# Two 192-slot experts in a mixture-of-experts decoder: high and low token halves in one 128-column stationary

## The reference

```
logits = (x2d @ router_w).astype(jnp.float32) + router_b.astype(jnp.float32)
top_val, top_idx = lax.top_k(logits, TOP_K)        # TOP_K = 2 of 8
gates = jax.nn.softmax(top_val, axis=-1)
...
    return swiglu(xb, w_gate[e], w_up[e], w_down[e])   # silu(h @ gate) * (h @ up) @ down
...
out = jnp.zeros((n + 1, d), ys.dtype).at[slot_tok].add(ys)
```

## Time and profile before

| what | value |
|---|---|
| median of 3 runs | 1949.5 us (1949.02 to 1953.09) |
| profiled execution | 1946.6 us, its span 1945.0 us |
| busy share of the span | PE 91%, PEld 81%, DVE 53%, ACT 40%, POOL 24% |
| mean granted TensorE clock over the span | 0.948 of full speed |
| first expert matmul, last store of an expert's rows | 1342.0 us, 1915.1 us |

### The profile page before, as it was taken

The page is one execution under the profiler, slowest core; times in us unless marked ns, Lnnn a source line. Parts: engine busy times, 40 slices in busy tenths (PEclk is TensorE's granted clock), DMA queues, the critical chain, the costliest instruction groups (busy, mean ns, idle before and its releaser), DMA issues.

```text
span 1945.0 us, 29426 instructions
## 1 busy us (share of the span) xinstructions
PE 1761.2 (91%) x10972; PEld 1582.8 (81%) x10972; DVE 1027.2 (53%) x1427; ACT 784.4 (40%) x1116; POOL 470.0 (24%) x1201
## 2 busy tenths in 40 slices
PE   5798998998999999998899889964999999999993
PEld 4688897998999999998777777743888888888882
DVE  5556544635333233325565546444755945855785
ACT  4244424223232232223244234224644744754773
POOL 5867881002000000006678840010000000000001
PEclk8798999998999999998879899996999999999997
DMA  3521222247223222224312222318956965975994
GB/s 120 99 69 52 69 66 74 86 133 271 87 86 96 88 88 87 95 86 136 67 48 79 66 77 76 121 33 325 355 176 213 374 232 187 368 248 180 336 370 174
DMA packets 124091, 291.35 MB, mean 150 GB/s; under 512 B 31024, under 2 KB 31152, under 8 KB 123840
## 3 DMA queue, kind: packets, MB, share of 16 engines
q1 hardware_dynamic: 90576, 241.38, 36.1%
q0 software_dynamic: 9376, 33.07, 4.7%
q10 hardware_dynamic: 24016, 15.25, 3.7%
HBM read 261.14 MB, written 28.51 MB: 149 GB/s over the span
## 4 chain that ended last, share of the span: by engine, by line
PE 76%; DVE 8%; ACT 5%; issue 5%; DMA 3%; ACTq 2%; POOL 0%; SPq 0%; POOLq 0%; DVEq 0%
PE acc L1511 39%; PE acc L1748 9%; PE acc L1749 8%; PE acc L1750 8%; PE side L1511 2%; PE side L1595 2%; PE acc L1541 1%; ACTq L814 1%; DMA uu<-u_d 1%; ACT wh L670 1%; DMA xg_d<-hn_tok,idx 1%; PE side L1519 1%; DVE rs L1037 1%; PE side L1793 1%; PE side L1618 1%
## 5 line engine op out<-in xcount | busy, mean ns | idle before, releaser
L1019 DVE TENSOR_TENSOR mwl<-mraw,mwh 128x1024 fp32r<-128x1024 f32 x288 | 338.1, 1221 | 117.4 <-ACT mwh L934 116.1
L1511 PE MATMUL acc<-xh,wh 128*128 128x264 f32 (+1 forms) x1600 | 381.8, 309 | 5.6 <-DVE wl L1019 2.5
L1511 PE MATMUL acc<-xl,wh 128*128 128x264 f32 (+1 forms) x1600 | 373.4, 303 | 0.0
L1511 PE MATMUL acc<-xh,wl 128*128 128x264 f32 (+1 forms) x1600 | 371.8, 302 | 0.0
L1019 DVE TENSOR_TENSOR wl<-raw,wh 128x512 fp32r<-128x512 f32 x328 | 217.9, 706 | 267.2 <-ACT wh L670 262.5
L934 ACT ACTIVATE mwh<-mraw 128x1024 fp32r<-128x1024 f32 x288 | 288.6, 1054 | 100.6 <-PE acc L1750 86.4
L1511 PEld LDWEIGHTS acc<-xh,wh 128*128 128x128 f32 x1600 | 260.6, 191 | 25.9 <-issue 11.8
L1511 PEld LDWEIGHTS acc<-xl,wh 128*128 128x128 f32 x1600 | 259.5, 191 | 10.4 <-issue 1.2
L1511 PEld LDWEIGHTS acc<-xh,wl 128*128 128x128 f32 x1600 | 258.6, 191 | 10.2
L670 ACT ACTIVATE wh<-raw 128x512 fp32r<-128x512 f32 x328 | 187.4, 621 | 186.7 <-PE acc L1511 143.2
L1748 PE MATMUL acc<-mwh,xth 128*128 128x512 f32 x528 | 208.4, 395 | 7.3 <-ACT ytok L980 4.8
(11 more groups left out here) (345 smaller groups left out, 2789.2 us busy)
## 6 DMA issues: line engine op xcount, KB each, us to landing
mraw<-in_W SPq DMA_DIRECT2D x288, 512.0 KB, 5.2
raw<-in_W SPq DMA_DIRECT2D x328, 256.0 KB, 2.7
xg_d<-zero POOLq DMA_DIRECT2D x15, 512.0 KB, 9.8
xt<-xg_d POOLq DMA_DIRECT2D x11, 512.0 KB, 6.9
yg_d<-ytok POOLq DMA_DIRECT2D x11, 512.0 KB, 3.7
hs<-in_xT SPq DMA_DIRECT2D x8, 264.0 KB, 4.7
u_d<-uperm ACTq DMA_DIRECT2D x8, 264.0 KB, 2.0
uu<-u_d ACTq DMA_DIRECT2D x16, 132.0 KB, 6.5
```

What stands on the lines that cost most here:

```text
L1019: return v.tensor_tensor(out, a, b, op)
L1511: ins = mm(out, w, x[:, t0:t1], start=first and i == 0, stop=last and i == 2)
```

## The change

Ranks 1 and 2 get 192 slots instead of 256: a full tile and a half tile of 64 tokens (HALF). rows_in(b, t) tells a tile's rows. In the half tile the low parts lie in columns 64 to 127 of xth and hth, beside the high parts in columns 0 to 63, so that one 128-column stationary holds both. The sums of rows 64 to 127 (low part times high weights) belong to the tokens of rows 0 to 63, and are added to them later, on the way to silu, to hb and to ytok. The routing arithmetic follows the new capacities, and up to five extra tiles (was four) can follow.

```diff
-CAPS = tuple(n * TOK for n in NT)
+HALF = TOK // 2
+CAPS = (2 * TOK, TOK + HALF, TOK + HALF) + (TOK,) * (EXPERTS - 3)
-EXTRA = 4
-SLOTS = (TILES + EXTRA) * TOK
+EXTRA = 5
+FIRST_EXTRA = sum(CAPS)
+SLOTS = FIRST_EXTRA + EXTRA * TOK
...
+        part = place("part", [HALF, 2, HCOLS], at=[UU()[0], UU()[1]])
+        def rows_in(b, t):
+            return min(TOK, CAPS[ORDER[b]] - t * TOK) if isinstance(b, int) and b < EXPERTS else TOK
...
@@ gpsimd @@
+                    pool.dma_start(xt[0:n, t, :], rows(xg_d, at + t * TOK, n)).then_inc(xt_landed[t], 16)
...
@@ scalar @@
+                            if r == HALF:
+                                a.activation(part[:, 0, :], acc[HALF:TOK, 0, 1, :], ACT.Copy).then_inc(upper_ready, 1)
+                                act.wait_ge(part_ready, halves_before(b) * CH + c + 1)
+                            a.activation(sg[0:r, x, :], part[:, 0, :] if r == HALF else acc[:, 0, t, :], ACT.Silu)\
+                                .then_inc(silu_ready, 1)
+                    if j in MUL_AT and rows_in(b, nt - 1) == HALF:
+                        arrived(j)
+                        a.activation(part[:, 1, :], acc[HALF:TOK, 1, 1, :], ACT.Copy).then_inc(upper_ready, 1)
...
+                    if rows_in(b, t) == HALF:
+                        arrived(U_MOE - 1)
+                        a.activation(ytok[0:HALF, x, :].rearrange("p (b c) -> p b c", b=2), moe_sums(nt, t)[HALF:TOK],
+                                     ACT.Copy).then_inc(upper_ready, 1)
+                        continue
...
@@ vector, routing @@
-            v.tensor_scalar(baseE[k], rankE[k], float(WIDE), float(TOK), ALU.min, ALU.mult)
-            link(v.tensor_scalar(capE[k], rankE[k], float(WIDE), float(TOK), ALU.is_lt, ALU.mult))
+            v.tensor_scalar(baseE[k], rankE[k], 3.0, float(HALF), ALU.min, ALU.mult)
+            v.tensor_scalar(xtmp[k], rankE[k], 1.0, float(HALF), ALU.min, ALU.mult)
+            v.tensor_scalar(capE[k], rankE[k], 3.0, float(HALF), ALU.is_lt, ALU.mult)
+            link(v.tensor_scalar(extra[k], rankE[k], 1.0, float(HALF), ALU.is_lt, ALU.mult))
+            tt(baseE[k], baseE[k], xtmp[k], ALU.add)
+            link(tt(capE[k], capE[k], extra[k], ALU.add))
...
+            v.tensor_scalar(incl[k], xtmp[k], float(2 * TOK), 0.0, ALU.is_gt, ALU.add)
             link(tt(extra[k], extra[k], ebase[k], ALU.add))
+            link(tt(extra[k], extra[k], incl[k], ALU.add))
...
@@ vector, expert blocks @@
+                low = xtl[:, t, :, :] if r == TOK else xth[:, t, :, HALF:TOK]
...
+                    if j in SILU_AT and rows_in(b, nt - 1) == HALF:
+                        dve.wait_ge(upper_ready, halves_before(b) * (2 * CH + 1) + SILU_AT.index(j) * 2 + 1)
+                        tt(part[:, 0, :], part[:, 0, :], acc[0:HALF, 0, 1, :], ALU.add).then_inc(part_ready, 1)
...
+                            if r == HALF:
+                                dve.wait_ge(upper_ready, halves_before(b) * (2 * CH + 1) + c * 2 + 2)
+                                link(tt(part[:, 1, :], part[:, 1, :], acc[0:HALF, 1, 1, :], ALU.add))
+                            tt(hb[0:r, x, :], sg[0:r, x, :], part[:, 1, :] if r == HALF else acc[:, 1, t, :], ALU.mult)\
+                                .then_inc(hidden_ready, 1)
...
+                if rows_in(b, nt - 1) == HALF:
+                    x = (tb + 1) % 2
+                    dve.wait_ge(ytok_ready, tb + 1)
+                    dve.wait_ge(upper_ready, (halves_before(b) + 1) * (2 * CH + 1))
+                    y2 = ytok[0:HALF, x, :].rearrange("p (b c) -> p b c", b=2)
+                    tt(y2, y2, moe_sums(nt, 1)[0:HALF], ALU.add).then_inc(ytok_ready, 1)
...
@@ tensor @@
+                    ins = nc.tensor.transpose(side[:, m // 4, m % 4 * P:m % 4 * P + r], xt[0:r, t, m * P:(m + 1) * P],
+                                              ident[0:r, 0:r])
...
-                def product(out, w, cols, hi, lo, first, last):
-
+                def product(out, w, cols, hi, lo, r, first, last):
+
+                    if r == HALF:
+                        if first:
+                            mm(out, hi, mwh[w][:, cols], start=True, stop=False)
+                        ins = mm(out[0:HALF], hi[:, 0:HALF], mwl[w][:, cols], start=False, stop=False)
+                        return ins if first else mm(out, hi, mwh[w][:, cols], start=False, stop=last)
                     mm(out, hi, mwh[w][:, cols], start=first, stop=False)
                     mm(out, lo, mwh[w][:, cols], start=False, stop=False)
                     return mm(out, hi, mwl[w][:, cols], start=False, stop=last)
```

More of the change, by code:

```diff
@@ L513, in _ @@
                         pool.dma_start(xg_d[z:z + n, :], zero[0:n, :]).then_inc(zeroed, 16)
-                    for z in range(TILES * TOK, SLOTS, P):
+                    for z in range(FIRST_EXTRA, SLOTS, P):
                         n = min(P, SLOTS - z)
@@ L608, in _, with rows @@
             pool.wait_ge(scattered, 2 * TB * 16)
-            def rows(d, at):
-                return d[at:at + TOK, :] if isinstance(at, int) else d[bass.ds(at, TOK), :]
+            def rows(d, at, n=TOK):
+                return d[at:at + n, :] if isinstance(at, int) else d[bass.ds(at, n), :]
             def load(b, tb, nt, at):
@@ L617, in load @@
                 for t in range(nt):
-                    pool.dma_start(xt[:, t, :], rows(xg_d, at + t * TOK)).then_inc(xt_landed[t], 16)
+                    n = rows_in(b, t)
+                    pool.dma_start(xt[0:n, t, :], rows(xg_d, at + t * TOK, n)).then_inc(xt_landed[t], 16)
             load(0, 0, NT[ORDER[0]], BASE[ORDER[0]])
@@ L625, in _ @@
                     pool.wait_ge(ytok_ready, tb + t + 1)
-                    pool.dma_start(rows(yg_d, BASE[ORDER[b]] + t * TOK), ytok[:, (tb + t) % 2, :])\
+                    n = rows_in(b, t)
+                    pool.dma_start(rows(yg_d, BASE[ORDER[b]] + t * TOK, n), ytok[0:n, (tb + t) % 2, :])\
                         .then_inc(y_stored[(tb + t) % 2], 16)
@@ L631, in _ @@
                 with pool.Fori(0, n_extra) as i:
-                    at = i * TOK + TILES * TOK
+                    at = i * TOK + FIRST_EXTRA
                     pool.wait_ge(xt_turned, i + TILES)
@@ L934, in wide_hi_of, with gather_hi @@
                 a.activation(mwh[w][:, :], mraw[j % RAWS][:, :], ACT.Copy).then_inc(wide_hi[w], 1)
-            def gather_hi(n, t):
+            def gather_hi(n, t, r=TOK):
                 act.wait_ge(xt_turned, n + 1)
-                a.activation(xth[:, t, :, :].rearrange("p (b k) s -> p b (k s)", b=2), side[:, 0:2, :], ACT.Copy)\
+                a.activation(xth[:, t, :, 0:r].rearrange("p (b k) s -> p b k s", b=2),
+                             side[:, 0:2, :].rearrange("p b (k s) -> p b k s", k=4)[:, :, :, 0:r], ACT.Copy)\
                     .then_inc(xth_ready, 1)
@@ L963, in moe_block @@
                             act.wait_ge(hidden_turned, n + 1)
-                            a.activation(hth[:, t, 4 * c:4 * c + 4, :].rearrange("p k s -> p (k s)"), side[:, 2 + x, :],
+                            r = rows_in(b, t)
+                            a.activation(hth[:, t, 4 * c:4 * c + 4, 0:r],
+                                         side[:, 2 + x, :].rearrange("p (k s) -> p k s", k=4)[:, :, 0:r],
                                          ACT.Copy).then_inc(hth_ready, 1)
@@ L1381, in _ @@
             link(v.tensor_scalar(ebase[k], xtmp[k], float(TOK), 0.0, ALU.is_gt, ALU.add))
+            v.tensor_scalar(incl[k], xtmp[k], float(2 * TOK), 0.0, ALU.is_gt, ALU.add)
             link(tt(extra[k], extra[k], ebase[k], ALU.add))
+            link(tt(extra[k], extra[k], incl[k], ALU.add))
             link(v.tensor_tensor_scan(incl[k], oneE[k], extra[k], 0.0, ALU.mult, ALU.add))
             link(tt(ebase[k], incl[k], extra[k], ALU.subtract))
-            link(v.tensor_scalar(xtmp[k], ebase[k], float(TOK), float(TILES * TOK), ALU.mult, ALU.add))
+            link(v.tensor_scalar(xtmp[k], ebase[k], float(TOK), float(FIRST_EXTRA), ALU.mult, ALU.add))
             link(tt(xtmp[k], xtmp[k], capE[k], ALU.subtract))
@@ L1419, in wide_lo_of, with gather_lo @@
                 tt(mwl[w][:, :], mraw[j % RAWS][:, :], mwh[w][:, :].bitcast(F32), ALU.subtract).then_inc(wide_lo[w], 1)
-            def gather_lo(n, t):
+            def gather_lo(n, t, r=TOK):
                 dve.wait_ge(xth_ready, n + 1)
-                as2 = lambda x: x[:, t, :, :].rearrange("p (b k) s -> p b (k s)", b=2)
-                tt(as2(xtl), side[:, 0:2, :], as2(xth).bitcast(F32), ALU.subtract).then_inc(xtl_ready, 1)
+                as2 = lambda x: x.rearrange("p (b k) s -> p b k s", b=2)
+                low = xtl[:, t, :, :] if r == TOK else xth[:, t, :, HALF:TOK]
+                tt(as2(low), side[:, 0:2, :].rearrange("p b (k s) -> p b k s", k=4)[:, :, :, 0:r],
+                   as2(xth[:, t, :, 0:r].bitcast(F32)), ALU.subtract).then_inc(xtl_ready, 1)
             def moe_block(b, tb, nt, nxt, slack=1):
```

(10 more changed lines are left out.)

27 lines of the change are left out of this document (15 added, 12 removed).

## The result

The kernel after takes 1928.4 us (median of 4 runs, 1922.7 to 1930.5) against 1951.3 for the kernel before in the same comparison: ratio 0.9875, 95% interval 0.9858 to 0.9892. Timed again with five runs, it was 1922.9 us and 0.9851 (0.9835 to 0.9867). It is faster by 1.2 to 1.5%, 23 to 28 us; 14 us slower was forecast.

A forecast was written before the change was run, and what follows sets the result against it. TensorE, busy 91% of the span, was taken as the bound. A block: -16.3 + 21.1 + 1.1 + 0.74 = +6.6; twice 13.3, plus routing 0.75, gave +14.0 us: median 1963.5, range 1918 to 1977.

The forecast's parts named there:

- Part 2: Touched expert blocks: each trip from 128x128 to 128x64 stationary and back drains TensorE, 0.35 us; 66 trips, 21.1 us a block.
- rival A: Changing the stationary's width alone drains nothing in the touched blocks: 27.4 us less in all, 1922 us; chance 0.20.
- Rival B: At width changes weight loads are exposed but nothing drains: 8.6 us a block for 21.1, total 1938.5; chance 0.06.
- Part 1: Half tile of the touched blocks: 72 matmuls of 0.2265 us go, saving 16.3 us a block.
- part 5: Block's end: with drains, remaining matmuls cover the first tile's ytok copy; without, PE waits 0.4 us. DVE's add costs nothing.
- Part 3: Half tile's transposes: four groups a block with 64x128 stationaries, entered and left, cost 1.1 us; being narrower gains nothing.
- Part 4: Folding the low rows' sums: gate sums hidden; at the last hb PE resumes later, 0.74 us more a block.
- Part 6: Routing arithmetic before the scatter: extra DVE steps add 0.75 us, all of which shows.

The follow-up runs named there:

- cols32: The kernel after with its narrow pass cut to 32 columns (tokens 32 to 63 lose their low-weight pass); 1922.3 us, one run.

## Why the prediction was wrong, point by point

**Part 2 is the step that failed.** It said: "So the array changes its shape by the size of the stationary alone, even at partition 0, in the direction of rows. I take it that columns do the same." The first sentence is right, and its price of a trip was near (0.32 worked out, 0.334 measured), in part by luck, as the control below shows. The second is wrong: 128x64 beside 128x128 costs 0.011 us a pass, not 0.32 a trip. So 21.1 us a block were charged where 0.8 was paid, 42 in all for 1.6, and with them the sign changed. Every row that it rested on changed rows; none changed columns alone, and rival A named just that. With 0.20 it had too little (and the chance of a faster kernel adds up to 0.29 from the terms given, not 0.27), since no row spoke for the step from rows to columns; the Trainium skill's rule did the rest. The Trainium skill (TensorEngine Tiling (Array Packing), Key Properties and its list of configurations) counts 128x64 as a mode and has mode changes drain the array; the run with 64 rows agrees, the kernel after at 128x64 and cols32 at 128x32 do not, and the measurement decides. Whether the page would count a 64-column stationary beside full ones as that mode, no run can tell. Rival B, loads exposed without a drain, is out as well, since no load of the narrow passes is exposed. The time lies inside the stated range only because the range was drawn out to rival A.

**Part 1** (16.3 a block) is right: the 15.85 measured are 16.3 less the wait of 0.46 at the block's end, for which part 5 had 0.4 in this case.

**Part 3** had the half transposes at 1.1 a block. The kernel after shows them, first the tokens' and then a group of hb (four full, four half), and last, from the kernel before, the matmul behind the eight full ones of the earlier trace rows:

```profile
1555.95 0.71 PE L1792 MATMUL side<-ident,xt 64*128 64x64 f32 x8
1556.59 0.50 PE L1805 MATMUL acc<-mwh,hth 128*128 128x512 f32 x1
...
1586.55 0.99 PE L1851 MATMUL side<-ident,hb 128*128 128x128 f32 x8
1587.47 0.49 PE L1805 MATMUL acc<-mwh,xth 128*128 128x512 f32 x1
...
1580.95 0.48 PE L1748 MATMUL acc<-mwh,xth 128*128 128x512 f32 x1
```

Eight half ones and the way back take 0.64, where eight full ones take 0.79: they do get faster when they are narrower (eight in 0.71 for 1.03, so 0.06 apart and not 0.11), against what the prediction said of the load, and that pays for the drain at their two ends. The three groups of hb take 0.92 for 0.79, 0.39 us a block. The tokens' 0.15 less falls in the one-tile block before, so 0.24 us are left for both, and 0.39 in the touched block.

**Part 4** is right in mechanism and nearly in size: copy, add and hb follow as written, 0.84 more for 0.74. **Part 5**: the 0.4 of the case without a drain came, 0.44; the add into ytok (1.2 us) held up no matmul. **Part 6**: from the rank reduction to the first scatter it was 8.96 us (1296.88 to 1305.84) and is 9.64 (1306.53 to 1316.17), 0.68 more for 0.75.

With the drain of the narrow passes taken out, the sum of a touched block is -16.3 + 0.8 (narrow passes) + 0.39 + 0.84 + 0.44 = -13.8, for -13.74 measured. Two such blocks give 27.5; less the 0.5 of block 0 and small differences, that is the stage's 26.8, and less the routing's 0.7 it is 26.1. Rival A (27.4 less, 1922 us) is what the kernel does (1928.4 and 1922.9). Its nearness is helped by two errors that offset each other: 1.1 for the transposes where 0.39 was paid, and nothing for the narrow passes where 0.8 was.

The mixer of the kernel before holds a control for the earlier trace rows: the same place without the 64x64 matmuls, 128x128 behind 128x128, with the same wait at the head of the unit (the waits of the 64x64 matmuls are absent).

```profile
228.46 0.39 PE L1618 MATMUL side<-sr,m2y 128*128 128x66 f32 x2
228.57 0.28 PE L1618 MATMUL side<-sr,m2y 128*128 128x66 f32 x1
228.65 0.49 PE L1511 MATMUL acc<-xh,wh 128*128 128x264 f32 x2
...
228.62 0.30 PEld L1511 LDWEIGHTS acc<-xh,wh 128*128 128x128 f32 x2
```

The load starts 0.05 behind the last small matmul and runs beside it, so on the way out the shape and not the wait held it back; of the way in the control says nothing. It also corrects the price. The second of the two L1511 matmuls starts at 228.86 (228.65 + 0.49 - 0.28), 0.21 behind the first and not the 0.12 that Part 2 took as usual. Counted as in Part 2, its first one would be 0.06 late with no change of shape at all, and so much of the 0.20 going out was not the drain. Rows and columns it does not part; only a run could.

## What to carry to other kernels

When a cost is read from a row in which two things change at once, the row does not say which of them is paid for, and "only the other one matters" belongs in the forecast at its full weight. In the stream measured here (512 moving columns, narrow output at partition 0), a stationary with fewer columns among full ones is nearly free (0.011 us a pass) and gains nothing; fewer contraction rows cost a drain and an exposed load at each change. Putting the low halves beside the high ones in one stationary saves one of three passes of the half tile (16.3 us a block here), and the fold costs little (0.84 where PE waits for it), less still if what waits for it is given other work first.

## What the runs showed of the hardware

- A change between 64 and 128 rows in the stationary, and back, costs 0.334 us at 64 columns and 0.389 at 128 (0.400 against the kernel with full width), matmuls of 512 columns; the load at each change starts only with its own matmul. A second 64-row matmul behind the first pays nothing. Between 128x128 and 128x64 or 128x32 loads run ahead as always. All with the narrow shape at the array's first rows and columns; other positions were not run.
- A 128x64 stationary makes its pass 0.011 us longer than a 128x128 one does (88.20 against 87.42 over 72 passes).
- Eight float32 transposes with stationaries of 64x128 stand 0.06 us apart (0.71 in all), with 128x128 0.11 (1.03 in all), though both stationaries have 128 columns.
- The touched blocks of the kernel after repeat within 0.02 us from profile to profile and the other blocks behind block 0 within 0.1, while whole runs of one kernel lie 11 us apart. Block 0 varies with the length of its start at the lower clock (55.25 us in the kernel before, 55.78 and 55.60 in the kernel after). What this change does is read from the windows far more sharply than from the medians.
